# A hybrid decoder step: four stages joined to one, with the decode's page groups between the dense products

## The reference, cut to what matters

```python
def mixer_inputs(x, mod, w_in, cos, sin):
    z = modulate(x, mod[:, 0], mod[:, 1]) @ w_in
    h, gb, gc, q, k, v = jnp.split(z, SPLIT_IDX, axis=-1)
    # rotary on the first 16 of each 64 dims of q and k

mod = adaln(c, w_ada, b_ada)                     # silu(c) @ w_ada + b_ada, 6 parts of 1024
u_ext = concat([state, gc * h]); y_conv = gb * short_conv(u_ext, conv_w)
p = softmax(q k^T / 8), two components per head  # causal for the prompt; all past and new keys for the samples
o = (p[:, :, 0] - lam * p[:, :, 1]) @ v
xp = finish(x, concat([y_conv, head_out(o)]), mod, w_out, ln1, w_gate, w_up, w_down, ln2)
```

## Time and profile before

| | us |
|---|---|
| median of 3 runs | 2384.13 |
| lowest, highest | 2380.84, 2389.08 |
| span of the profiled execution | 2380.2 |

### The profile page before, as it was taken

How to read it: one execution, slowest core, us unless ns; L and a number is a source line. 1 busy time by engine, 2 the same in 40 slices (tenths; PEclk the granted TensorE clock), 3 DMA queues, 4 the chain that set the end, 5 groups by cost and what they waited for, 6 DMA issues and landing times.

```text
span 2380.2 us, 47877 instructions
## 1 busy us (share of the span) xinstructions
PE 1984.2 (83%) x17492; PEld 1635.0 (69%) x17492; DVE 1056.3 (44%) x1528; ACT 486.3 (20%) x831; POOL 354.0 (15%) x544
## 2 busy tenths in 40 slices
PE   4699999668786876878785794999999997999992
PEld 1277898557665765767674793777777776888881
DVE  2424211666675665766561557111111112455457
ACT  0300111021212112121221203111211111333331
POOL 0000000223242423324232104200000000000003
PEclk7799999799897988889796896999999998999996
DMA  9711223779897979879896410121212123411112
GB/s 302 256 36 35 72 71 118 250 245 341 285 385 282 385 279 346 314 283 381 298 354 234 156 35 18 54 71 53 88 53 70 53 88 128 137 41 37 36 32 91
DMA packets 210968, 404.21 MB, mean 170 GB/s; under 512 B 24426, under 2 KB 88938, under 8 KB 210788
## 3 DMA queue, kind: packets, MB, share of 16 engines
q1 hardware_dynamic: 161012, 261.51, 31.9%
q0 software_dynamic: 41488, 136.35, 15.5%
q10 hardware_dynamic: 8320, 4.19, 0.6%
HBM read 377.53 MB, written 24.51 MB: 169 GB/s over the span
## 4 chain that ended last, share of the span: by engine, by line
PE 65%; DVE 13%; SPq 7%; DMA 7%; issue 6%; ACT 1%; DVEq 0%; ACTq 0%
PE psum L753 26%; PE psum L1002 11%; PE psum L761 10%; PE psum L852 5%; DVE k_turned L1432 4%; SPq L445 4%; SPq L449 3%; DMA ada_w<-w_ada 3%; DMA k_ring<-cache_k 3%; PE psum L1009 2%; PE psum L862 2%; DVE p_t L424 2%; PE psum L736 2%; PE psum L832 1%; DVE x_lo L1282 1%
## 5 line engine op out<-in xcount | busy, mean ns | idle before, releaser
L852 PE MATMUL psum<-k_turned,q_blocks 128*32 128x128 f32 x4096 | 332.3, 286 | 85.6 <-DVE k_turned L1432 84.9
L852 PEld LDWEIGHTS psum<-k_turned,q_blocks 128*32 128x32 f32 x4096 | 291.7, 114 | 137.1 <-issue 98.5
L1432 DVE STREAM_TRANSPOSE k_turned<-k_ring 128x2048 f32<-128x2048 f32 x128 | 295.4, 2308 | 6.6 <-DMA k_ring<-cache_k 5.7
L753 PE MATMUL psum<-x_hi,w_hi 128*128 128x512 f32 x896 | 281.3, 395 | 0.0
L753 PE MATMUL psum<-x_lo,w_hi 128*128 128x512 f32 x896 | 277.3, 391 | 0.0
L753 PE MATMUL psum<-x_hi,w_lo 128*128 128x512 f32 x896 | 276.0, 389 | 0.0
L1301 DVE TENSOR_TENSOR w_lo<-w_raw,w_hi 128x2048 fp32r<-128x2048 f32 x37 | 86.9, 2350 | 363.1 <-ACT w_hi L1057 353.5
L1002 PE MATMUL psum<-d_hi,h_hi 128*128 128x256 f32 x704 | 209.2, 297 | 12.2 <-DVE d_lo L1646 11.1
L862 PE MATMUL psum<-v_ring,p_t 128*32 128x128 f32 x4096 | 191.7, 295 | 19.3 <-DMA v_ring<-cache_v 18.9
L1002 PE MATMUL psum<-d_lo,h_hi 128*128 128x256 f32 x704 | 199.9, 284 | 0.0
L1002 PE MATMUL psum<-d_hi,h_lo 128*128 128x256 f32 x704 | 199.7, 284 | 0.0
(11 more groups left out here) (228 smaller groups left out, 2525.1 us busy)
## 6 DMA issues: line engine op xcount, KB each, us to landing
k_ring<-cache_k SPq DMA_DIRECT2D x256, 256.0 KB, 8.0
k_ring<-cache_k POOLq DMA_DIRECT2D x256, 256.0 KB, 6.1
v_ring<-cache_v SPq DMA_DIRECT2D x256, 256.0 KB, 8.8
v_ring<-cache_v POOLq DMA_DIRECT2D x256, 256.0 KB, 6.0
ada_w<-w_ada SPq DMA_DIRECT2D x12, 2048.0 KB, 9.6
w_raw<-w_in SPq DMA_DIRECT2D x12, 1024.0 KB, 5.3
w_raw<-w_gate SPq DMA_DIRECT2D x11, 1024.0 KB, 5.4
w_raw<-w_up SPq DMA_DIRECT2D x11, 1024.0 KB, 6.3
```

Of the source, the lines that this page charges most:

```text
L753: last = mm(psum[:, 2 * ft + c, 0:CH], w[:, s, k, ft * P:(ft + 1) * P], x[:, k, c * CH:(c + 1) * CH], start=k == 0 and j == 0, stop=k == K ...
L852: last = mm(psum[QUAD * h:QUAD * (h + 1), g % 2, 0:GP * QUAD], q_blocks[:, h, d, :], k_turned[:, g % 2, :, h * HD + d * QUAD:h * HD + (d + ...
L1432: v.transpose(k_turned[:, g % 2].rearrange("p j n -> p (j n)"), k_ring[:, g].rearrange("p j n -> p (j n)")).then_inc(k_free, 1)
```

## The change

Stages 1 to 3 become one stage; what follows is the same but for a few places in the buffers, the order of the low part of the first output weights (it now stands behind the splitting of y) and a second load of the samples' x. In the joined stage nothing loops: a Python function `walk()` lists steps, and every engine's stream is written out by going through that list. Its parts:

- Only the first 4 of 12 modulation blocks (shift and scale of the input) stand ahead of the products. The other 8 come between the token pairs of blocks 0 to 3. `w_ada` comes in halves of 1 MB. The gates go through DRAM (`gates_store`) and are read back with the bias during attention; SP issues these loads.
- The input projection takes q, k, v first (6 blocks by token, in pairs of tiles that share two PSUM banks), then the six convolution blocks by feature, each pass of 128 columns in two halves. The convolution is kept for 256 channels at a time and stored.
- The low part of a weight block is written over the raw weights (`in_lo` in the place of `in_raw`), so the samples' product of a block comes before its low part is made.
- Decode slots are put between all these: 1.25 per piece in blocks 0 to 4, 2.5 per piece in blocks 5 to 11 (22 and 70 slots), 1.5 per tile in attention (48), and 4 at the end. There are 144: 16 per sequence and 16 more, as the values of a sequence run one sequence behind its keys. Values of a sequence start in slot 5: two groups in each of slots 5 to 9, one in each of 10 to 15 (`values_at`).
- The rings hold two groups each in place of four, and there is one `k_turned` in place of two. POOL issues all key pages, SP all value pages.
- The matmuls of a key group run over d outside and heads inside, before it was the other way round. The scores of the prompt multiply 64 rows per component, before they multiplied 128 with one half zero, and both components are done together for the maxima.
- Weights of the decode are turned in two halves (after slots 3 and 4); ScalarE regroups the first half, VectorE the second.

```diff
-        k_ring = ar("k_ring", [P, RING, GP, AW])
-        v_ring = ar("v_ring", [P, RING, GP, AW])
-        k_turned = place("k_turned", [P, 2, GP, AW], F32, ar.at)
+        in_hi = ar("in_hi", [P, 2, KC, WB], F32R)
+        in_raw_at = ar.at
+        in_raw = ar("in_raw", [P, 2, KC, WB])
+        in_lo = place("in_lo", [P, 2, KC, WB], F32R, in_raw_at)
...
+        v_ring = ar("v_ring", [P, 2, GP, AW])
+        k_ring = ar("k_ring", [P, 2, GP, AW])
+        k_turned_at = ar.at
+        k_turned = ar("k_turned", [P, GP, AW])
...
+        ada_w = place("ada_w", [P, 4, KC // 2, BANK], F32, v_ring_at)
+        x_rows = place("x_rows", [P, NT, D], F32, k_turned_at)
...
-                with eng.Fori(0, REVS) as r:
-                    for g in range(par, RING, 2):
-                        group(*keys, b + 1, r, g)
-                        group(*values, b, r, g)
-            with eng.Fori(0, REVS) as r:
-                for g in range(par, RING, 2):
-                    group(*values, B - 1, r, g)
...
+        values_at = [[]] * 5 + [[2 * i, 2 * i + 1] for i in range(5)] + [[i] for i in range(10, 16)]
+            def decode(count):
+                owed[0] += count
+                while owed[0] >= 1.0:
+                    owed[0] -= 1.0
+                    b, i = next(slots, (None, None))
+                    if b is None:
+                        return
+                    order.append(("keys_and_values", b, i))
+                    if b and i in (3, 4):
+                        turned[b, i - 3] = pair(None if under_way[0] is None else 1 - under_way[0])
+                        order.append(("weights", b, i - 3) + turned[b, i - 3])
+                    if b and values_at[i]:
+                        order.append(("values", b, i, turned[b, 0], turned[b, 1]))
+                    if b > 1 and i == 2:
+                        order.append(("sample_head", b - 2))
...
+            ada = iter(range(ADA_FIRST, ADA))
+            for n in range(NB_IN):
+                rate = 1.25 if n < 5 else 2.5
+                if n < BY_TOKEN:
+                    for p in range(NT // 2):
+                        order.append(("tokens", n, p) + pair())
+                        if p == 0 and n:
+                            order.append(("rope", n - 1))
+                        if n == 0 and p == 0:
+                            order.append(("first_queries",))
+                        if p == 1 and n:
+                            order.append(("store", n - 1))
+                        if n < 4:
+                            if p % 2 == 0:
+                                a = next(ada)
+                                order.append(("ada", a))
+                            else:
+                                order.append(("ada_fold", a))
+                        if n and p == 1:
+                            order.append(("sample", n + 1))
+                        if n and p == 2:
+                            order.append(("sample_fold", n + 1))
+                        if n == 4 and p == 0:
+                            order.append(("first_values",))
+                        if n or p > 1:
+                            decode(rate)
...
+                else:
+                    for ft in range(FT):
+                        at = pair()
+                        for half in range(2):
+                            order.append(("features", n, ft, half) + at)
+                            under_way[0] = at[0] if half == 0 else None
+                            if n == BY_TOKEN and ft == 0:
+                                order.append((("rope", "store")[half], n - 1))
...
+                            decode(rate)
...
+            order.append(("attention_loads",))
+            order.append(("fetch_head", 0))
+            behind = None
+            for n in range(H * NT):
+                h, i = n // NT, n % NT
+                if i == 0:
+                    order.append(("turn_keys", h) + pair())
+                    order.append(("turn_queries", h) + pair())
+                    if h + 1 < H:
+                        order.append(("fetch_head", h + 1))
+                order.append(("scores", n, pair(0), pair(1)))
+                decode(0.75)
+                order.append(("combine", n))
+                if n:
+                    behind = pair()
+                    order.append(("turn_rows", n - 1) + behind)
+                decode(0.75)
+                if n:
+                    order.append(("weigh", n - 1) + behind)
+                if n == 1:
+                    order.append(("sample_conv",))
+                if n == 8:
+                    order.append(("gates",))
+            behind = pair()
+            order.append(("turn_rows", H * NT - 1) + behind)
+            decode(1.0)
+            order.append(("weigh", H * NT - 1) + behind)
+            decode(1000.0)
+            order.append(("sample_head", B - 1))
+            return order
...
+            def load_values(n):
+                for j in range(GP):
+                    page = sp.value_load(page_row[0:1, n * GP + j:n * GP + j + 1], min_val=0, max_val=z.POOL - 1)
+                    sp.dma_start(v_ring[:, n % 2, j, :], v_pages[ds(page, 1)].rearrange("o p d -> p (o d)")
+                                 ).then_inc(v_in[n % 2], 16)
...
+                elif what == "values":
+                    b, i = at[0:2]
+                    for g in values_at[i]:
+                        n = (b - 1) * GROUPS + g
+                        if n + 2 < B * GROUPS:
+                            sp.wait_ge(values_done, n + 1)
+                            load_values(n + 2)
...
+                elif what == "block_end":
+                    n, = at
+                    if n + 2 < NB_IN:
+                        sp.wait_ge(dense_done, blocks_done(n))
+                        load_in(n + 2)
...
+            for n in range(B * GROUPS):
+                for j in range(GP):
+                    page = pool.value_load(page_row[0:1, n * GP + j:n * GP + j + 1], min_val=0, max_val=z.POOL - 1)
+                    if j == 0 and n >= 2:
+                        pool.wait_ge(turned_keys, n - 1)
+                    pool.dma_start(k_ring[:, n % 2, j, :], k_pages[ds(page, 1)].rearrange("o p d -> p (o d)")
+                                   ).then_inc(k_in[n % 2], 16)
+            pool.wait_ge(stage_done, 4)
...
-                for h in range(H):
-                    for d in range(4):
-                        last = mm(psum[QUAD * h:QUAD * (h + 1), g % 2, 0:GP * QUAD], q_blocks[:, h, d, :],
-                                  k_turned[:, g % 2, :, h * HD + d * QUAD:h * HD + (d + 1) * QUAD],
-                                  start=d == 0, stop=d == 3)
-                last.then_inc(scored, 1)
+                n = b * GROUPS + i
+                if i == 0:
+                    pe.wait_ge(q_ready, b + 1)
+                pe.wait_ge(turned_keys, n + 1)
+                if n:
+                    pe.wait_ge(scores_kept, n)
+                for d in range(4):
+                    for h in range(H):
+                        last = mm(psum[QUAD * h:QUAD * (h + 1), KEYS, 0:GP * QUAD], q_blocks[:, h, d, :],
+                                  k_turned[:, :, h * HD + d * QUAD:h * HD + (d + 1) * QUAD], start=d == 0, stop=d == 3)
+                last.then_inc(scored, 1)
...
+            for a in range(ADA_FIRST):
+                ada(a)
+                if a:
+                    ada_fold(a - 1)
+            ada_fold(ADA_FIRST - 1)
...
+                act.wait_ge(dense_done, 4 * n + p + 1)
+                if n == 0 and p == 0:
+                    act.wait_ge(x_in_split, UNITS)
+                    act.wait_ge(xs_in_turned, 1)
+                if n >= 2 and p == 0:
+                    act.wait_ge(z_stored[n % 2], 16 * (n // 2))
+                copy(z_rows[:, n % 2, 2 * p:2 * p + 2, :], psum[:, 2 * x:2 * x + 2, 0:WB]).then_inc(pair_free[x], 1)
...
+            def keep_quads(n):
+                dve.wait_ge(in_s_done, n + 1)
+                v.tensor_copy(in_quads[:], psum[:, MISC, 0:WB]).then_inc(misc_free, 1)
+                in_misc[0] += 1
+                dve.wait_ge(in_hi_done, n + 1)
+                v.tensor_tensor(in_lo[:, n % 2], in_raw[:, n % 2], in_hi[:, n % 2], ALU.subtract).then_inc(in_lo_done, 1)
...
+            def turn_keys(n):
+                dve.wait_ge(k_in[n % 2], 16 * GP * (n // 2 + 1))
+                if n:
+                    dve.wait_ge(scored, n)
+                v.transpose(k_turned[:].rearrange("p j n -> p (j n)"), k_ring[:, n % 2].rearrange("p j n -> p (j n)")
+                            ).then_inc(turned_keys, 1)
...
+                for k0 in range(0, (i + 1) * P, BANK):
+                    w = min(BANK, (i + 1) * P - k0)
+                    for c in range(2):
+                        last = mm(psum[:, 2 * c + k0 // BANK, 0:w], q_t[c * QK:(c + 1) * QK, h % 2, i * P:(i + 1) * P],
+                                  k_t[c * QK:(c + 1) * QK, h % 2, k0:k0 + w], start=True, stop=True)
```

(1 more changed line is left out.)

1636 lines of the change are left out of this document (913 added, 723 removed).

## The result

| | us |
|---|---|
| before, median of 4 runs (lowest, highest) | 2382.49 (2379.52, 2389.08) |
| after, median of 4 runs (lowest, highest) | 2530.84 (2523.20, 2533.37) |
| ratio after / before, 95% interval | 1.061 [1.0586, 1.0633] |
| span of the profiled execution after | 2529.0 |
| forecast (range) | 2190 (2085 to 2350) |

The change makes the kernel 148 us slower. The forecast had the wrong sign, and its range left the result out. Its span was 2186 us, so there are 343 us to account for.

A forecast was written before the change was run, and what follows sets the result against it. Decode was taken as bound by DMA page loads, input projection by TensorE, and put side by side: 69 + 185 + 450 + 27 + 377 = 1108 us against 1305, 3 more later, so 2190 us (range 2085 to 2350).

The forecast's parts named there:

- The step that failed: Slots in blocks 5 to 11: set by issues or DMA at 4.9, 9.8 or 5.4 us, with dense products hidden.
- hand-over: Between block 11 and attention: SP's read-back of values and head 0 plus 27 small loads, 27 us.
- the 199: Blocks 5 to 11: forecast at 450 us, measured 649, off by 199.
- margin of the issues: Page issues in blocks 5 to 11: unrolled code may save a register operation per page, 20 us taken off.
- regrouping: Copies of decode weights ahead of a transposition: 6.7 us, of which 4 us exposed in each of four sequences, 16.
- Rival C: Blocks 5 to 11: loads and products do not overlap, so 28 half passes add 157 us, time 2347; chance 0.18.
- Rival D: Value ring on SP: pages landing after 11 us make 7.8 us per group, time 2457, slower than before; chance 0.11.
- The attention: Attention and end of decode: 32 tiles with a chain of 8.7 us and 1.5 slots each, 377 us in all.
- wrong altogether: Sign against the whole forecast: waits for ScalarE or VectorE copies above 150 us, where it priced 16.
- The clock: Dense products in blocks 5 to 11: a lower TensorE clock works like rival C; granted 0.89 in decode before, no price.
- Start and blocks 0 to 4: First input product after 69 us, then the five projection blocks with 22 page groups, 185 us.
- The late part: Everything behind attention and decode: 1075 us before, nearly unchanged, plus 3 us for a later weight split.

The follow-up runs named there:

- kernel with pages: Changed kernel with feature passes in four pieces (1.25 slots after each), one value group a slot, value and key rings handled page by page: 2342.29 us.
- experiment 1: Changed kernel with two of three feature products left out in blocks 6 to 11: 2482.74 us (-48); its other kernels load one page of four.
- a quarter of the pages: Changed kernel loading one page of four in each key and value group after the first two groups: 2271.03 us (-260).
- experiment 4: Key products with parts outside and heads inside on the kernel before: 2376.06 us; the reverse order on the changed kernel: 2600.60 us.
- experiment 2: Changed kernel with each queue issuing every second group of keys and of values, rings unchanged: 2634.14 us (+103).

## Why the prediction was wrong

**The step that failed** is "so slots without values last 4.9 us, slots with two value groups 9.8 (SP), slots with one are set by the DMA, 5.4", together with "the dense products of these blocks lie under the loads". The slot lengths were a queue's issue time or the DMA's transfer time, as if the queues issued all the time. But a ring of two groups is full after two groups. During a product piece of 5.7 to 7.8 us no buffer comes free, so a queue stands as soon as its two groups are loaded (POOL for 14.89 us in the timeline above, SP for some 4), and in the burst behind it each slot after the first pays its issues and its landing in a row. Measured from one key product to the next over the 70 slots that I had counted there, product pieces included: 20 without values last 7.4 us on average, 24 double 12.6, 26 single 7.6 when the hand-over of 23 us in the last of them is taken off (4.9, 9.8 and 5.4 in the forecast). That makes 175 us. The other 24 of the 199 are what I had taken off the sum: 20 for groups loaded ahead and 20 as margin of the issues, with 16 added for regrouping. Issues were indeed faster, 1.09 and 1.13 us, and it gave nothing. By the experiments: bursts 67, double slots 75, latency of a group through the ring 62 to 69, and they add for the most part, 2530.8 - 2342.3 = 189 us. By the traces 137 of these lie ahead of attention, 53 in it. The kernel with pages is still 152 us above the forecast; what holds those isn't shown beyond the parts below.

**Rival C** (loads and products don't overlap) had this mechanism, "rings of two are full after one slot", and priced it at 157 us for the feature blocks. I set against it that a half pass is as long as one group's loading. That is true of the first slot of a burst and says nothing of the other 1.5. By experiment 1 the exposure of the products themselves was about half, 48 of 87 us. Its sign, slots plus products adding up, came nearer to the truth than the forecast: the 24 feature pieces took 160 us.

**Rival D** (slower than before, at the value ring on SP) had the sign and the place. Its condition, over 7.0 us per value group where values limit, was nearly met and not quite: double slots took 6.3 a group, single ones 7.6, 6.8 on average. Its price hung on long landings, though, and these were 4.1 us at the median. What made the turn of a buffer long was that nothing asks for the page until a group is used. The tests that I had named for D, landings over 9 us and waits over 300, would have ruled it out.

**The attention**, +107 us. A tile's chain was taken at 8.7 us with 5.8 per slot. With a quarter of the pages the stretch from the first score product to the last value product is 390 us, and in the changed kernel 477 (forecast 377 without the turn into it): so some 90 us are the same loads, and the chain's own length was near. The kernel with pages has 424. TensorE's longest wait there apart from pages is for the exponentials (changed kernel, 290 to 1446 us; the group of before had no idle time, L825 in the earlier trace rows):

```profile
L1048 PE MATMUL psum<-consts,a_rows 128*128 128x128 f32 x144 | 32.8, 376 | 76.3 <-ACT e_rows L1302 76.3
```

With a quarter of the pages it is as long (that run's waits: us in total, times, longest):

```profile
PE psum L1048 <- ACT e_rows L1302: 75.2, 26, 7.6
```

So it is no part of what the loads cost; it belongs to the chain that I had summed at 8.7 us a tile. With the softmax of decode and the copies all of TensorE's waits for ScalarE and VectorE, the transposed keys apart, come to some 159 us in the changed kernel and 152 in that run, past the 150 that I had named for "wrong altogether" and far over the 16 that I had priced. Yet that run comes within 83 us of the forecast's span: these waits lay mostly in chains that the sum held under other names, and they aren't what made the 343 us.

**The clock.** The granted clock in the feature blocks is 0.77 and in the attention 0.71, against 0.89 in the decode of before. A value group takes 1.94 us at the low level and 1.05 to 1.08 at the high one. In the feature blocks 35 of the 40 key and value groups that came behind a wait of over 2 us took more than 1.6 us, and 15 of the 70 behind no wait. The 24 feature pieces took 6.7 us on average where I had 5.6, 25 us together. I had named the clock in half a sentence of rival C and given it no number. How much of the 343 us is the clock can't be told from these runs, as the edits that took waits away raised it too (0.852 over the whole kernel, 0.891 with quarters, spread values and pages). The Trainium skill ("TensorE: Matmul & The Clock Gate", "HAM oscillation — how this bites in real kernels") says that waits for DMAs between matmuls drop the clock; the trace agrees, with the 35 of 40 groups above.

**Start and blocks 0 to 4**, +12 and +24. The first input product came at 80.7 us. The 16 units of x take one after the other 1.3 us each (ScalarE's read-out, a cast and a subtraction), 55.3 to 76.0, some 21 us where I had 17; that is 4 of the 12. For the rest, and for the 24, I ran nothing.

**What held.** The key products at 0.9 us a group from start to start at the high clock (762.50 to 763.40 us in the timeline above), worth 70 us here (experiment 4); at the low one they take 1.9. The hand-over, 23 for 27. The late part, within 5. Regrouping, 6.93 us for 16 copies on VectorE and 6.0 on ScalarE against 6.7. The queues' cadence, 1.13 us a page on POOL and 1.09 on SP where I took 1.22: faster, and of no use, since the queues stood half of the time. One kind of page per queue, against half of both (experiment 2). The 20 us that I had left out of the sum for key loads held up by VectorE didn't show: POOL's 512 issues of keys lasted 537 to 617 ns with a median of 539. The Trainium skill's rule ("SBUF — State Buffer", "SBUF: two separate sides") says that such a DMA waits for a VectorE copy or tensor_scalar between SBUF operands in the two-port mode. Seven issues ran beside the scalings of attention's rows; they lasted 617 ns at most, and their pages landed after 4.2 us at the median and 6.2 at most (the others 4.5 and 12.3). No run shows whether these scalings ran in that mode.

**The signs.** Of those that I had named for "right" only the key groups under 1.2 us held, and at the high clock alone. The first input product came at 80.7 us (65 to 75 expected), slots took 7.4 and 12.6 (5 and 10), the DMA moved 248 GB/s in blocks 5 to 11 (290 to 330), and the stage ended at 1446 (1080 to 1140).

## What to carry to other kernels

A queue's cadence is a slot's length only if the queue never stops: with rings of n groups, count what happens to the queues in the longest stretch in which the consumer doesn't use a buffer, and give each use in the burst behind it issues plus landing unless the ring holds the whole burst. When two stages are merged on one in-order engine, spread the loads' uses evenly, in pieces no longer than the ring covers, hand buffers back page by page, and only then ask whether the merge pays: here the plain merge cost 148 us and the one with quarters, spread values and pages gained 43. Check the merge by shifting its share-out: if the loads' strand ends at the same time for 2, 2.5 and 3 slots per piece, its own pace is the bound, and the share-out should let both strands end together.

## What the hardware showed that I had not expected

- TensorE's time taken away or added went with the clock. In the kernel before, with 107 us less of matmuls in decode, the granted clock was 0.78 in place of 0.89, and 8 us of time were won. In the changed kernel, with 190 busy us more, it was 0.886 over the whole kernel in place of 0.852.
- Two queues with half of both kinds each are worse than one kind per queue by 103 us, at equal bytes and equal rings: SP stood for 397 us at key buffers, and TensorE's wait for values rose from 190 to 311 us.
- Transposing a group page by page costs VectorE little: 0.67 us a page (ns 656/670/715), 2.7 us a group against 2.31 in one, 321.1 us in all against 295.6. Handing over by pages more than paid for it.
